# Query norms on four column groups, and GpSimd at the start of a streaming encoder step

## What is computed

```python
h = rmsnorm(x, norm_mix)                    # needs sum(x*x) over 1024 channels
P = h @ w_in                                # pool, window attention, latents, gates
qm = (rmsnorm(q_lat) @ mla_w_qup)           # 8 heads of 96 (64 plain + 32 rotary)
qm = rmsnorm(concat(plain, rope(rotary)), mla_qk_q_norm)   # <- sums per head and token
km, vm = expand(latents of cache and new, mla_w_kvup)      # keys are normed too
y_mla = softmax(qm @ km.T / sqrt(96), chunk-causal) @ vm
y_pool, y_swa = pooling mixer, window attention (8 heads, 2 key heads, band 192)
x += (sum_i sigmoid(gate_i) * (y_i @ w_branch_i)) @ w_out
x += SwiGLU(rmsnorm(x)) 
```

## Time and profile before

| what | us |
|---|---|
| median of three runs | 1062.59 |
| the profiled execution | 1062.87 |
| its span, first to last instruction | 1061.1 |
| TensorE busy | 1051.5 (99%) |
| VectorE busy | 631.3 (59%) |
| ScalarE busy | 504.6 (48%) |
| GpSimd busy | 304.8 (29%) |

### The profile page before, as it was taken

The page is one execution under the profiler, slowest core; times in us unless marked ns, Lnnn a source line. Parts: engine busy times, 40 slices in busy tenths (PEclk is TensorE's granted clock), DMA queues, the critical chain, the costliest instruction groups (busy, mean ns, idle before and its releaser), DMA issues.

```text
span 1061.1 us, 20088 instructions
## 1 busy us (share of the span) xinstructions
PE 1051.5 (99%) x7630; PEld 1012.5 (95%) x7630; DVE 631.3 (59%) x1059; ACT 504.6 (48%) x887; POOL 304.8 (29%) x224
## 2 busy tenths in 40 slices
PE   8999999999999999999999999999999999999998
PEld 6899998999999999999988999989999999999998
DVE  6768555545766665643577784644467565656444
ACT  7455655534554434434354475544445544343342
POOL 2366555551121111000122755456312111111000
PEclk9999999999999999999999999999999999999999
DMA  7455433344445444454514453333444354454543
GB/s 252 119 146 156 124 101 112 108 120 144 154 120 170 155 150 146 150 178 146 175 43 134 145 145 105 120 120 101 120 150 153 120 173 150 146 156 141 159 147 122
DMA packets 48770, 147.92 MB, mean 139 GB/s; under 512 B 8480, under 2 KB 13952, under 8 KB 48704
## 3 DMA queue, kind: packets, MB, share of 16 engines
q1 hardware_dynamic: 42576, 144.69, 43.7%
q10 hardware_dynamic: 6128, 2.30, 0.9%
HBM read 143.75 MB, written 3.22 MB: 139 GB/s over the span
## 4 chain that ended last, share of the span: by engine, by line
PE 93%; DVE 4%; ACT 2%; POOL 1%; issue 0%; DMA 0%; SPq 0%; POOLq 0%; DVEq 0%; ACTq 0%
PE psum L499 28%; PE psum L500 27%; PE psum L501 27%; PE psum L647 1%; PE psum L686 1%; POOL ssum L1772 1%; PE psum L669 1%; PE psum L677 1%; PE psum L718 1%; PE psum L891 1%; PE psum L611 1%; PE psum L606 0%; DVE kT L1669 0%; PE psum L628 0%; PE psum L769 0%
## 5 line engine op out<-in xcount | busy, mean ns | idle before, releaser
L499 PE MATMUL psum<-AH,WH 128*128 128x320 f32 x1328 | 416.5, 314 | 0.2
L501 PE MATMUL psum<-AH,WL 128*128 128x320 f32 x1328 | 411.2, 310 | 0.0
L500 PE MATMUL psum<-AL,WH 128*128 128x320 f32 x1328 | 411.1, 310 | 0.0
L499 PEld LDWEIGHTS psum<-AH,WH 128*128 128x128 f32 x1328 | 249.9, 188 | 7.7 <-issue 5.5
L500 PEld LDWEIGHTS psum<-AL,WH 128*128 128x128 f32 x1328 | 250.0, 188 | 0.7
L501 PEld LDWEIGHTS psum<-AH,WL 128*128 128x128 f32 x1328 | 249.9, 188 | 0.0
L966 ACT CAST WH<-raw 128x1024 fp32r<-128x1024 f32 x173 | 180.5, 1046 | 141.1 <-PE psum L501 139.8
L1777 POOL TENSOR_TENSOR WL<-raw,WH 128x1024 fp32r<-128x1024 f32 x65 | 159.3, 2461 | 172.1 <-ACT WH L966 136.4
L1358 DVE TENSOR_TENSOR WL<-raw,WH 128x1024 fp32r<-128x1024 f32 x106 | 131.6, 1243 | 122.8 <-ACT WH L966 122.5
L1530 DVE TENSOR_TENSOR WL<-raw,WH 128x1024 fp32r<-128x1024 f32 x88 | 107.6, 1222 | 49.5 <-ACT WH L1126 48.2
L1782 POOL TENSOR_TENSOR fab<-fa,fb 128x320 f32<-128x320 f32 x44 | 38.6, 877 | 270.2 <-DVE fb L1535 270.2
(11 more groups left out here) (237 smaller groups left out, 1549.9 us busy)
## 6 DMA issues: line engine op xcount, KB each, us to landing
raw<-w_all SPq DMA_DIRECT2D x267, 512.0 KB, 3.5
y_out<-X SPq DMA_DIRECT2D x8, 160.0 KB, 2.9
X<-x_in SPq DMA_DIRECT2D x2, 320.0 KB, 5.6
X<-x_in SPq DMA_DIRECT2D x1, 640.0 KB, 7.4
lat_out<-ckv ACTq DMA_DIRECT2D x2, 320.0 KB, 2.8
scratch<-brel SPq DMA_DIRECT2D x8, 63.8 KB, 4.3
ckv<-lat_in SPq DMA_DIRECT2D x1, 384.0 KB, 4.7
bias<-scratch SPq DMA_DIRECT2D x8, 48.0 KB, 4.8
```

What stands on the lines that cost most here:

```text
L499: mm(out, WH[:, slot, c0:c0 + cols], high, start=first, stop=False)
L500: mm(out, WH[:, slot, c0:c0 + cols], low, start=False, stop=False)
L501: return mm(out, WL[:, slot, c0:c0 + cols], high, start=False, stop=last)
```

## The change

**Query sums.** The squares become the moving operand: one matmul per head over all 320 tokens, with a stationary matrix `pick` of 32 columns in which one column is ones. Head h goes to the 32 partitions of column group h % 4, rows 0 or 1 of it by h // 4, and the two rounds accumulate in the same columns of bank 3. The first round stands in the middle of gate 1 instead of behind gate 0, the second behind gate 1 as before. The root is taken over all of it into sqm[:, 0]; ten matmuls per layer with a selection of identity columns (`turn_sums`, behind the transposes of window item 1) turn it to 20 columns of bank 3, and VectorE takes the reciprocal from there in item 2. `turn` of item 2 instead of item 0 waits for that.

**Order around it.** The squares of a group of heads come ahead of a weight cast on ScalarE. The reciprocal `rw` of the window queries moves behind the four yPL subtractions.

**Layer 0's start.** GpSimd casts units 2 and 3, which ScalarE did before; ScalarE makes the squares 0 to 3 there, GpSimd adds them earlier, and TensorE does the sum ahead of the rotary columns, as in layer 1.

**Layer 1's start.** AL[6] and AL[7] move from key block 1 to key block 3.

```diff
-            if l > 0:
-                stat_mix(l, 0)
+            stat_mix(l, 0)
             rope_columns(l)
-            if l == 0:
-                stat_mix(l, 0)
...
+        def query_sums(l, g):
+            pe.wait_ge(s.pick_ready, 1)
+            pe.wait_ge(s.sq_mq, 8 * l + 4 * g + 4)
+            for h in range(4 * g, 4 * g + 4):
+                last = mm(psum[32 * (h % 4):32 * (h % 4) + 32, 3, 64:64 + T], pick[0:QK, 31 - h // 4:63 - h // 4],
+                          sqm[0:QK, h % 4, :], start=g == 0, stop=g == 1)
+            last.then_inc(s.mq_stat, 4)
+        def turn_sums(l):
+            pe.wait_ge(s.mq_sums, l + 1)
+            heads = ident.rearrange("p (g e r) -> p r e g", g=2, e=2)[:, 0:2]
+            for b in range(5):
+                for hq in range(2):
+                    out = psum[hq * 64:hq * 64 + 64, 3, b:20:5].rearrange("p (r g) -> p r g", r=2)
+                    last = mm(out, sqm[:, 0, b * 64:b * 64 + 64], heads[:, :, hq, :], start=True, stop=True)
+            last.then_inc(s.mq_turned, 1)
...
-            for g in range(2):
-                gate(l, g)
-                for h in range(4 * g, 4 * g + 4, 2):
-                    pe.wait_ge(s.sq_mq, 8 * l + h + 2)
...
+            gate(l, 0)
+            gate(l, 1, between=lambda: query_sums(l, 0))
+            query_sums(l, 1)
...
                 turn(l, i)
+                if i == 1:
+                    turn_sums(l)
...
             for g in range(2):
+                query_squares(l, g)
                 high(l, U_GATE + g + LEAD)
...
-            A(rq[:], psum[:, 3, 0:20], ACT.Sqrt, scale=1.0 / QK, bias=eps).then_inc(s.mq_root, 1)
+            A(sqm[:, 0, :], psum[:, 3, 64:64 + T], ACT.Sqrt, scale=1.0 / QK, bias=eps).then_inc(s.mq_sums, 1)
...
                 elif l == 0 and kb < 3:
-                    high(l, U_KV + kb - 1)
+                    norm_chunk(l, 0, 2 * kb - 2, high=False)
+                    norm_chunk(l, 0, 2 * kb - 1, high=False)
...
+            if l == 0:
+                high(l, U_KV)
             for kb in range(CACHED):
                 rope_keys(l, kb)
                 if l == 0 and kb == 0:
                     low(l, U_KV)
+                elif l == 0 and kb == 1:
+                    high(l, U_KV + 1)
+                    sum_squares(l, 0, 1, 2)
+                elif l == 0 and kb == 2:
+                    sum_squares(l, 0, 2, 4)
             if l == 0:
-                sum_squares(l, 0, 1)
+                sum_squares(l, 0, 4)
```

More of the change, by code:

```diff
@@ L1069, in gate_tanh, with query_squares @@
             A(G[:, g, :], G[:, g, :], ACT.Tanh, scale=0.5).then_inc(s.gate_ready, 1)
+        def query_squares(l, g):
+            for h in range(4 * g, 4 * g + 4):
+                act.wait_ge(s.tile_free, l * NT + T_Q + h + 1)
+                if h >= 4:
+                    act.wait_ge(s.mq_stat, 8 * l + 4)
+                A(sqm[0:QK, h % 4, :], Q[0:QK, h, :], ACT.Square).then_inc(s.sq_mq, 1)
         def softmax_exp(l, i):
@@ L1174, in _ @@
                     norm_chunk(l, 0, k, square=False)
-                for k in range(KC):
+                for k in range(4, KC):
                     norm_chunk(l, 0, k, high=False)
-                    if k == 3:
+                    if k == 5:
                         key_columns(l, CACHED - 1)
+                act.wait_ge(s.high_ready, U_KV + 2)
             else:
@@ L1540, in _ @@
         v.memset(par[:, DEPTH * NPAR:(DEPTH + 1) * NPAR], 0.0).then_inc(s.x_ready, KC)
+        v.memset(pick[:], 0.0).then_inc(s.pick_zero, 1)
+        dve.wait_ge(s.pick_zero, 1)
+        v.memset(pick[:, 31:32], 1.0).then_inc(s.pick_ready, 1)
         cached_low(0, 0)
@@ L1555, in _ @@
                     norm_low(l, 0, kb)
-                elif kb < 2:
-                    norm_low(l, 0, 4 + 2 * kb)
-                    norm_low(l, 0, 5 + 2 * kb)
+                elif l == 0 and kb == 2:
+                    norm_low(l, 0, 2)
+                    norm_low(l, 0, 3)
                 elif kb == 2:
[L1560 to L1564, removed]
+                    low(l, U_KV + 1)
+                elif l > 0 and kb in (0, 3):
+                    norm_low(l, 0, 4 + 2 * (kb // 3))
+                    norm_low(l, 0, 5 + 2 * (kb // 3))
             if l == 0:
@@ L1667, in _ @@
                     ALU.mult, ALU.subtract).then_inc(s.tile_free, 1)
+            dve.wait_ge(s.swq_root, l + 1)
+            link(l, v.reciprocal(rw[:], rw[:]))
             STT(kT[:, 0:SEQ], kT[:, 0:SEQ], col(C_SWK, l), stdk[:, 0, 0:SEQ], ALU.mult, ALU.mult)
@@ L1684, in _ @@
             gate_out(l, 1)
-            dve.wait_ge(s.mq_root, l + 1)
-            link(l, v.reciprocal(rq[:], rq[:]))
-            link(l, v.tensor_scalar(rq[:], rq[:], MSCALE, None, ALU.mult))
             dve.wait_ge(s.bias_in, 128)
@@ L1692, in _ @@
                 gate_out(l, 2 + 2 * i)
+                if i == 2:
+                    dve.wait_ge(s.mq_turned, l + 1)
+                    v.reciprocal(rq[:], psum[:, 3, 0:20]).then_inc(s.mq_root, 1)
+                    dve.wait_ge(s.mq_root, l + 1)
+                    link(l, v.tensor_scalar(rq[:], rq[:], MSCALE, None, ALU.mult))
                 gate_out(l, 3 + 2 * i)
```

27 lines of the change are left out of this document (15 added, 12 removed).

## The result

The changed kernel takes 1065.33 us (median of 14 runs, 1063.22 to 1067.4), the kernel before 1063.15 (14 runs). The ratio is 1.002, 95% interval [1.0013, 1.0026]: 2.2 us slower, where 4.0 us faster was forecast. 1065.33 lies above the range, which ended at 1061.6. One execution of the kernel before, at 1540 us and a granted clock of 0.62, is left out of all figures.

A forecast was written before the change was run, and what follows sets the result against it. TensorE, busy 99% of the span, was taken as the bound. Gains of 1.1 (sums), 0.5 (layer 1's start) and 2.4 (layer 0's start) made 4.0 off 1062.87, 1058.9; the median 0.28 lower, 1058.6 us; range 1056.8 to 1061.6.

The forecast's parts named there:

- The sums' matmuls: Query sums on TensorE: new blocks and turning take 2.12 us instead of 2.67 per layer, 1.1 gained in all.
- Rival (c): Query sums: column groups overlap only in pairs, total gain 1.8, 1060.8 us; chance 0.13, including 0.02 for running in sequence.
- my estimate of 0.85 for the block: Query sums: a block of four matmuls would take 0.85 us by the skill's share, making the gain 0.6 smaller.
- ScalarE's root ... where VectorE now reads it; 0: Query sums: the root over 320 columns ends long before VectorE reads it in the third item; cost 0.
- Layer 0's start, 2.4 gained: Layer 0's start: 1.90 from a shorter stretch at best, less 1.1 of lateness, plus 1.59 from the clock: 2.4 us gained.
- The 1.1 of lateness: Layer 0's start: GpSimd's fourth last sum ends at 31.8, TensorE ready at 30.7; 1.1 us given back in pieces.
- The clock's 1.59: Layer 0's start: the clock stays up, so twelve products take 1.86 instead of 3.45 us, 1.59 gained.
- (b): Layer 0's start: the 1.1 us stand in one piece, the clock falls; start gives 0.8, total 1060.2 us; chance 0.12.
- (d): Layer 0's start: a GpSimd cast costs 2.4 us like the split; 1.6 slower, 1064.2 us; chance 0.10.
- The yPL order, 0: yPL ahead of the reciprocal of rw: TensorE's wait moves and doesn't shrink; 0, at best 0.3 us a layer.
- Layer 1's start, 0.5: Layer 1's start: moving two AL operations removes the idle before block 2's keys and their longer transposes; 0.5 us gained.
- No wait for the second squares: Query sums in gate 1: second four squares ready at 119.7, wanted about 119.95, so TensorE doesn't wait; cover 0.2 us.

The follow-up runs named there:

- e10: Kernel before with the query sums' part, rq's operations in VectorE's idle time, and layer 1's AL move; layer 0's start and yPL order as before: 1061.26 us.
- e5: Changed kernel with rq's two operations exchanged in the same place: scaling reads PSUM, then reciprocal goes SBUF to SBUF: 1062.88 us.
- e8: Kernel before with the change's layer 0 start, but the rotary columns still ahead of the sum on TensorE: 1062.42 us.
- e9: Kernel before with only TensorE's order in layer 0 changed, the sum ahead of the rotary columns: 1066.33 us.
- e13: Changed kernel with rq's operations in VectorE's idle time, rotary columns ahead of the sum, and the old yPL order: 1059.40 us.
- e2: Kernel before with the change's layer 0 start alone, including the sum ahead of the rotary columns: 1065.43 us.
- e11: Changed kernel with rq's operations in VectorE's idle time and layer 0's rotary columns ahead of the sum; the change's yPL order stays: 1060.58 us.
- e1: Kernel before with the query sums' part of the change alone; both starts and yPL order as before: 1064.55 us.
- e3: Kernel before with layer 1's move of two of VectorE's AL operations alone: 1062.48 us.
- e7: Kernel before with the four yPL ahead of the reciprocal of rw alone: 1063.73 us.
- e4: Changed kernel with the reciprocal and scaling of rq ahead of the third item's softmax end on VectorE: 1067.82 us.
- e6: Changed kernel with rq's two operations moved to where VectorE idles and GpSimd does nothing: 1062.76 us.

## Why the prediction was wrong, step by step

- **The sums' matmuls** (2.67 to 2.12 us a layer): right. A block takes 0.68 (0.71 forecast), turning them 0.68 (0.70). Rival (c), column groups in pairs, is out. So is my estimate of 0.85 for the block. It carried over a share from the Trainium skill, "TensorE: Matmul & The Clock Gate", section "Measured speedup vs the span model", which has three column tiles in other shapes; the trace has 0.68. With rq's operations out of the way the two stretches give -1.2 + 0.55, 0.65 a layer against 0.55 forecast, and about 0.8 with the old yPL order (e10: 57.41 and 36.95).
- **"ScalarE's root ... where VectorE now reads it; 0"**: this step failed, and it costs 1.2 us a layer. I looked at whether the root is in time, and not at what the reader's two operations meet on VectorE's row. The evidence was in my own rows: kT, a VectorE operation, held for 2.41 us by a GpSimd split. Before, the scaling stood where GpSimd does nothing. The Trainium skill, "SBUF — State Buffer", section "Who interferes with whom", which I cited for two-input operations, also says that a `tensor_scalar` can take the shared port, and that the later of the two then blocks fully. The trace agrees (1.65 us, up to the split's end), and e5 shows the form that escapes: scaled from PSUM, and the reciprocal from SBUF.
- **Layer 0's start, 2.4 gained**: failed, 2.1 lost. Two terms of 1.90 - 1.1 + 1.59 were wrong, and one question wasn't asked.
  - **The 1.1 of lateness** was 3.16, and in one piece instead of several. Forecast for the sum's end was 31.8, measured 35.63, or 34.08 less the 1.55 us by which that execution is late at the first keys. The casts were near (1.15 forecast, 1.36 and 1.30 measured), and so was the start of the last four sums (27.1 forecast, 29.02 - 1.55 = 27.5). But I gave these four 4.7 us and they took 6.61. ScalarE makes only four squares there instead of eight and starts the next two weight casts earlier; VectorE's splits of them start 31.57 - 15.24 = 16.33 us behind the first key transposes (17.21 in the kernel before) and meet the last two sums again, as before. With the first sum beside the AL that makes three sums of 1.7, where I had 1.03 for each and 0.3 for meeting AL twice. No run moved the splits or these AL, so this part rests on the trace alone.
  - **The clock's 1.59.** In the old order a clock that stays up is worth 0.6 to 0.7, since the QL products at full clock run into a wait of 0.58 us (for the latent's low part), which the slow ones don't have. And in 37 of 52 executions it did not stay up; a fall now costs 2.8, which the sum had at nothing.
  - **The order.** 1.90 minus the lateness is the right form: 1.90 - 3.16 = -1.26, of which the later wait of 0.58, now gone, gives back nearly half, and the profiles have -0.6. The new order can pay only up to 1.9 us of lateness. What I never priced is the old order with the same earlier sum. There the columns, 2.4 us of work that needs no sum, are free up to the wait; behind it they cost their whole length. e8 has that kernel, 0.7 faster than before, and e9 has the order by itself, +3.2.
- **Rivals (b) and (d).** (b) named what happened in layer 0, the idle time in one piece and in most executions the clock down behind it, but priced it for 1.1 us of lateness, 0.8 gained. (d) had the sign of the whole and with 1064.2 nearly the time, but by a cast of 2.4; it came with casts of 1.3, so that match is luck.
- **The yPL order, 0**: small but on the other side, 0.1 to 0.15 a layer. The reciprocal of rw stood in a place where VectorE waited for ScalarE's yPH anyway (0.16 idle now) and now delays kT.
- **Layer 1's start, 0.5**: right, 0.64.
- **No wait for the second squares**: right, TensorE's list of waits has none.

By the parts run alone, the sum of 4.0 loses 2.3 at the query sums (1.1 forecast, -1.2 measured), 4.5 at layer 0's start and 0.5 at the yPL order, and gains 0.4 at layer 1's start: 2.9 slower, against 2.2 for the whole.

With rq's operations in idle time, and the columns and the yPL in their old order, the rest of the change gives 1059.4 (e13, five executions), where the forecast for the whole was 1058.6. It is another kernel, so this doesn't bear the forecast out.

## What to carry to other kernels

When an operation moves on an engine's row, look at what the neighbouring engine does at its new place, and at what the moved operation pushes there; here an operation of 0.17 us on VectorE lasted as long as the rest of GpSimd's split, 1.65. Work that doesn't need the late operand belongs ahead of the wait (e8 against e2), and an order copied from a place without a wait is no evidence for a place with one. A gain forecast for the clock has to be followed to the next wait, and one profile doesn't tell how often the clock falls.

## What the runs showed of the hardware

- **How often the clock falls, by the length of the wait for the sum.** It differs between executions of one kernel. Each execution has its mean granted clock, to three digits. Executions at 1.000: with a wait of 0.8 us (e8, e11, e13) 21 of 23; 2.1 us 46 of 139 (before 31 of 95; e1, e3, e7, e10 15 of 44); 3.1 us (after, e2, e4, e5, e6) 15 of 52; 4.4 us (e9) none of 9. The waits of 2.1 and 3.1 us can't be told apart by this; the shorter and the longer can. The kernel before itself had 15 of 31 in one group of runs and 7 of 27 in another. For the kernel before, the median is 1062.55 with the clock up and 1063.39 at 0.998.
- **Which VectorE operation a GpSimd split holds.** In the changed kernel: the scaling SBUF to SBUF, 20 columns, 1.65 instead of 0.18 (e6); two SBUF inputs, kT 2.43. Not held: a scaling from PSUM (0.17, e5), a reciprocal SBUF to SBUF (0.28, e5), gate rows with one input in PSUM (0.49).
- **Four column groups** of 32 run side by side: four matmuls of 320 float32 columns in 0.68 us, against 0.63 for a single full-width one.
- **GpSimd casts** 128x1024 float32 in 1.30 to 1.36 us, ScalarE in 1.04.
